# ScalarE's exponential table loaded among its input transfers, the lower bound served early, and the fourth projection tile in halves

## The chip, the cores and the metric

The kernel runs on one core of a Trainium2 chip. The metric is the device time of one execution in microseconds (us). TensorE (PE), VectorE (DVE), ScalarE (ACT), GpSimd (POOL) and SyncE (SP) each follow their own instruction stream and meet only at semaphores. Transfers are issued by SP, ScalarE and GpSimd, each on a queue of its own, and run on 16 shared DMA engines.

## What is computed

The reference is one layer of a decoder on 256 prompt tokens and 8 sample tokens (264 in all). The part that matters here is its head: a projection, and the forget gate made from one group of its columns.

```
proj = x @ w_in                      # (264, 2048) @ (2048, 10240), split into u v q f i g gate_a gate_b
p = softmax(lb_logits, axis=0); lower_bound = cumsum(p, axis=0) - p[0:1]
forget = lb + (1 - lb) * sigmoid(f)
logf = log(forget);  k = (1 - lb) * sigmoid(-f)
...                                  # gating, recurrence, output projections, norm,
...                                  # a mixture of 16 experts, norm
```

## The kernel before

**Arithmetic.** The input projection is computed as 80 column tiles of 128 columns ("tiles" below). Both operands are split into a high part in the reduced format fp32r and a low part, the rest. ScalarE makes the high part by a copy, VectorE the low part by a subtraction, and TensorE adds three products per block of 128 rows: high by high, high by low, low by high. With 16 blocks of rows (`KD`) a tile takes 48 matmuls of 264 columns, in `gemm_tile` (L662 to L664).

**The first three tiles** (`FIRST = 3`) go together, in seven chunks of rows given by `CUTS = (0, 2, 4, 6, 8, 10, 13, 16)`: five chunks of two blocks, two of three. SP issues the seven transfers of the weights (L419), ScalarE the seven of x (L1263). For each chunk ScalarE copies x (L1267), then the three tiles' weights (L1270); VectorE subtracts for x (L1464), then for the weights (L1467); TensorE waits for both and runs 18 or 27 matmuls (L843 to L845). TensorE has run 15 warm-up products before (L833).

**Tiles 3, 4, 5 and on.** SP issues each tile's weights as one transfer of 1 MB (L451), tiles 3 and 4 right behind the seven chunks, tile 5 and later ones only when TensorE has finished a tile (`gemm`). ScalarE makes the high part (`hi_part`, L1259), VectorE the low part (`lo_to`, L1455), and TensorE waits for the low part in `split_of`. Tiles 0 to 7 are the f group, whose results ScalarE takes out of the bank with two sigmoids each (L1293, L1294).

**The lower bound.** `lbl` is a parameter of 4 KB. GpSimd fetches it (L558), with two others, once all chunks of x are split (`xl_ready`). VectorE waits for all three, subtracts (L1472) and signals `lb_sub`; ScalarE answers with an exponential of 8 columns (L1320), behind the sigmoids of tile 1, and signals `lb_exp`. VectorE waits for it ahead of small set-up work (L1476 to L1484), which ends with the scales that the forget gates (L1489, L1490) and so the recurrence use. The compiler puts an ACT_TABLE_LOAD ahead of a function that the loaded table lacks.

**GpSimd** starts with masks and constants (L534 to L552) and then signals `consts`.

**Order.** Each engine's stream is written out by hand, and each engine follows its own strictly: an instruction that waits holds all behind it on that engine. Behind the projections come output projections, a norm, a router and the experts, whose weights SP streams through a ring as slots are freed.

Of the kernel before, what the change touches and what calls it, by code (L numbers as in the profile page):

```python
# [42 lines left out]
KD = D // P  # L43
# [58 lines left out]
def build(nc, x_t, w_in, ws_t, w00, b_s, lng, lnb, lbl, normg, state, woa, wob, wo, ln1g, ln1b, rw, rb,  # L102
          wg, wu, wd, ln2g, ln2b, y, st_p, st_s, v_s):
    with ExitStack() as ctx:
        def sem(name):
            return ctx.enter_context(nc.semaphore(name))
# [70 lines left out]
        def raw_of(q):  # L177

            return raw_early if q == FIRST + 1 else raw_w[q % 4]

        def lo_of(q):

            return lo_early[:, :] if q == FIRST + 1 else w_lo[q % 4][:, :]

        def chunk(buf, c):

            return buf.rearrange("p (k n) -> p k n", k=KD)[:, CUTS[c]:CUTS[c + 1], :]

        def chunk_of(buf, q, c):

            return buf[:, CUTS[c]:CUTS[c + 1], P * q:P * q + P]

        def raw_count(q):

            return q // 4 + (1 if q % 4 >= FIRST else 0)
# [79 lines left out]
        ones, _ = place("ones", [P, P])  # L275
        before = reg_qg[:, 2 * D:2 * D + P]
        quarter = before
        small, _ = place("small", [P, 648])
# [8 lines left out]
        lbw = take(4 * H).rearrange("p (a h) -> p a h", h=H)  # L287
# [6 lines left out]
        spare = take(3)  # L294
# [73 lines left out]
        x_in = [sem(f"x_in{q}") for q in range(CHUNKS - 1)]; side_in = sem("side_in"); par_in = sem("par_in"); ws_ready = sem("ws_ready"); ln1_in = sem("ln1_in"); router_in = sem("router_in")  # L368
# [4 lines left out]
        raw_in = [sem(f"raw_in{s}") for s in range(4)]; hi_ready = sem("hi_ready"); lo_ready = sem("lo_ready")  # L373
# [4 lines left out]
        lb_exp = sem("lb_exp"); lb_sub = sem("lb_sub")  # L378
# [14 lines left out]
        silu = sem("silu"); hid_ready = sem("hid_ready"); hid_tr = sem("hid_tr"); hid_ev = sem("hid_ev")  # L393
        ob_act = sem("ob_act"); ob_dve = sem("ob_dve"); weighted = sem("weighted"); pick_tr = sem("pick_tr"); pick_ev = sem("pick_ev")
        sc_mm = sem("sc_mm"); sc_ev = sem("sc_ev")
        early_mm = sem("early_mm"); early_ev = sem("early_ev"); half_in = x_in[0]; rows_in = sem("rows_in"); gain_mm = sem("gain_mm"); gain_ev = sem("gain_ev"); xg_ready = sem("xg_ready"); shift_ready = sem("shift_ready"); shift_mm = sem("shift_mm"); shift_ev = sem("shift_ev"); rank_two = sem("rank_two"); ya_ready = sem("ya_ready"); ln2q_in = sem("ln2q_in"); quarter_ready = sem("quarter_ready"); s_part = sem("s_part"); s_avg = sem("s_avg"); lob_act = sem("lob_act"); lob_dve = sem("lob_dve"); again = sem("again"); y_ready = sem("y_ready"); ys_ready = sem("ys_ready"); y_out = sem("y_out")
        zeroed = sem("zeroed"); dve_chain = sem("dve_chain")


# [16 lines left out]
        def _(sp):  # L416
# [22 lines left out]
            for q in range(FIRST, QUANTA):  # L439
                if q >= FIRST + 2:  # L440
                    sp.wait_ge(gemm, max(FIRST, tiles_done(q - 4)))
                if q < N_IN:
                    col = TILE_COL[q] * P
                    src, kk = w_in[:, col:col + P], KD
                elif q < N_IN + Q_OUT:
                    j = (q - N_IN) // 2
                    src, kk = (woa, wob)[(q - N_IN) % 2][:, 2 * P * j:2 * P * (j + 1)], H
                else:
                    j = q - N_IN - Q_OUT
                    src, kk = wo[:, P * j:P * (j + 1)], KD  # L450
                sp.dma_start(raw_of(q).rearrange("p (k n) -> p k n", k=kk),  # L451
                             src.rearrange("(k p) n -> p k n", p=P)).then_inc(raw_in[q % 4], 16)
                if q == N_IN + 8:

                    sp.dma_start(xt[:, :, :], x_t.rearrange("(k p) t -> p k t", p=P)).then_inc(x_again_in, 16)

                j = q - N_IN - Q_OUT
                if j >= 4 and j % 2 == 0 and j <= 12:
                    sp.wait_ge(gemm, N_IN + N_OUT)
                    first_unit((0, 2, 3, 4, 5)[j // 2 - 2])  # L460
# [65 lines left out]
        def _(pool):  # L526
            n = [0]
# [24 lines left out]
                link(pool.tensor_copy(out, iota_i[:, 0:k]))  # L552

            pool.nop().then_inc(consts, 1)

            pool.wait_ge(xl_ready, CHUNKS)
            with nc.allow_non_contiguous_dma("small parameters"):
                pool.dma_start(lbw[:, 0, :], lbl).then_inc(par_in, 16)  # L558
                pool.dma_start(ngain, normg).then_inc(par_in, 16)
                pool.dma_start(w00b, w00.partition_broadcast(P)).then_inc(par_in, 16)  # L560

# [86 lines left out]
        def _(pe):  # L648
            def gemm_tile(n, hi, lo, of_hi, of_lo):

                if n >= 4:
                    p = n - 4
                    if p < N_IN:
                        pe.wait_ge(act_evac, p + 1)
                    else:
                        pe.wait_ge(dve_evac, p - N_IN + 1)
                kk = len(hi)
                for k in range(kk):
                    if n == N_IN + N_OUT and k % 2 == 0:
                        pe.wait_ge(ml_ready, k // 2 + 1)  # L660
                    out = psum[n % 4][:, 0:T]
                    pe.matmul(out, hi[k], of_hi[:, k, :], start=(k == 0), stop=False)  # L662
                    pe.matmul(out, hi[k], of_lo[:, k, :], start=False, stop=False)  # L663
                    mm = pe.matmul(out, lo[k], of_hi[:, k, :], start=False, stop=(k == kk - 1))  # L664
                mm.then_inc(gemm, 1)
# [159 lines left out]

            def split_of(q, kk):

                pe.wait_ge(lo_ready, q + 1 - FIRST)
                return tuple(w.rearrange("p (k n) -> p k n", k=kk) for w in (hi_of(q), lo_of(q)))

            pe.wait_ge(warm, 1)
# [61 lines left out]
            for j in range(KD):  # L893
                n = N_IN + N_OUT + j
# [349 lines left out]
        def _(act):  # L1244
            evac_of = {}
            n = 0
# [5 lines left out]
            def hi_part(q):  # L1252

                if q < QUANTA:
                    if q >= FIRST + 2:
                        ahead = 3 if q < N_IN + Q_OUT + 2 else 2
                        act.wait_ge(gemm, tiles_done(q - ahead))
                    act.wait_ge(raw_in[q % 4], 16 * raw_count(q))
                    act.copy(hi_of(q), raw_of(q)).then_inc(hi_ready, 1)  # L1259

            for c in range(CHUNKS):
                part = slice(CUTS[c], CUTS[c + 1])
                act.dma_start(raw_x[:, part, :], x_t[P * CUTS[c]:P * CUTS[c + 1], :].rearrange("(k p) t -> p k t", p=P)).then_inc(x_in[c], 16)  # L1263
            for c in range(CHUNKS):
                part = slice(CUTS[c], CUTS[c + 1])
# [2 lines left out]
                act.wait_ge(first_in[c], 16)  # L1268
                for q in range(FIRST):
                    act.copy(chunk(hi_of(q), c), chunk_of(first_raw, q, c)).then_inc(first_hi, 1)  # L1270
            hi_part(FIRST)
            hi_part(FIRST + 1)
            def exps(lv):

# [13 lines left out]
            for n in range(N_IN):  # L1288
                name, j = evac_of[n]
                act.wait_ge(gemm, n + 1)  # L1290
                src = psum[n % 4][:, 0:T]
# [24 lines left out]
                    hi_part(n + 3)  # L1316
                if n == 1:
                    act.wait_ge(consts, 1)
                    act.wait_ge(lb_sub, 1)
                    act.activation(lbw[:, 1, :], lbw[:, 1, :], ACT.Exp).then_inc(lb_exp, 1)  # L1320
                if name == "q" and j == 3:
                    act.wait_ge(f_ready, 1)
                    act.activation(pcum[:, :, 0:NP_], pcum[:, :, 0:NP_], ACT.Ln).then_inc(logf, 1)
# [117 lines left out]
        def _(dve):  # L1441
# [8 lines left out]
            def lo_to(q_end):  # L1450

                while lo_next[0] <= min(q_end, QUANTA - 1):
                    q = lo_next[0]
                    dve.wait_ge(hi_ready, q + 1 - FIRST)
                    dve.tensor_tensor(lo_of(q), raw_of(q), hi_of(q).bitcast(F32), ALU.subtract).then_inc(lo_ready, 1)  # L1455
                    lo_next[0] += 1

            lo_next = [FIRST]
            dve.memset(ones[:, :], 1.0).then_inc(warm, 1)
            dve.memset(up[:, 0:4096 + 2 * H * BLK], 0.0).then_inc(zeroed, 1)  # L1460
            for c in range(CHUNKS):
                part = slice(CUTS[c], CUTS[c + 1])
                dve.wait_ge(xh_ready, c + 1)
                dve.tensor_tensor(x_lo[:, part, :], raw_x[:, part, :], x_hi[:, part, :].bitcast(F32), ALU.subtract).then_inc(xl_ready, 1)  # L1464
                for q in range(FIRST):
                    dve.wait_ge(first_hi, FIRST * c + q + 1)
                    dve.tensor_tensor(chunk_of(lo_first, q, c), chunk_of(first_raw, q, c), chunk(hi_of(q), c).bitcast(F32), ALU.subtract).then_inc(first_lo, 1)  # L1467
            lo_to(4)

            dve.wait_ge(par_in, 16 * 3)  # L1470
            dve.wait_ge(consts, 1)
            dve.tensor_tensor(lbw[:, 1, :], lbw[:, 0, :], lbw[:, 0, :], ALU.subtract).then_inc(lb_sub, 1)  # L1472
            dve.wait_ge(lb_exp, 1)
            for j in range(P // BLK):
                rows = slice(BLK * j, BLK * j + BLK)
# [192 lines left out]
            for r in range(Q_OUT):  # L1668
# [12 lines left out]
                for f in range(2):  # L1681
                    n = N_IN + 2 * r + f
# [37 lines left out]
            for j in range(KD):  # L1720
                n = N_IN + N_OUT + j
# [391 lines left out]
```

## Time and profile before

| | |
|---|---|
| median of 3 runs | 1659.89 us (1658.84 to 1660.66) |
| profiled execution, own time | 1660.23 us |
| its span on the core | 1658.5 us |
| TensorE busy | 1594.6 us (96%) |
| VectorE busy | 684.4 us (41%) |
| ScalarE busy | 392.1 us (24%) |
| GpSimd busy | 46.1 us (3%) |
| DMA | 543.87 MB, 328 GB/s on average |

The span is what the trace covers; the execution's own time is 1.73 us longer. Busy time of TensorE is modelled, since matmuls are pipelined, so 96% doesn't mean that it runs at its peak. Times in a timeline count from the span's start; what stands in brackets is the idle time of the engine just before the instruction, and what ended it.

### The profile page before, as it was taken

How to read it: one execution, taken by the hardware profiler on the slowest of the kernel's cores; microseconds unless marked ns; L12 is line 12 of the kernel's file. 1: busy time of each engine (PE TensorE's matmuls, PEld its weight loads, DVE VectorE, ACT ScalarE, POOL GpSimd, SP SyncE). 2: the span in 40 equal slices, each digit the busy share in tenths (PEclk: the TensorE clock that was granted, in tenths of full speed). 3: DMA queues.
4: the chain of work that ended last, by engine and by line, in shares of the span. 5: the costliest groups of instructions: out<-in, count | busy, mean ns of one | idle time of the engine just before them, and what ended most of it. 6: DMA issues, size and time to landing. Idle time of an engine off the chain costs nothing.

```text
span 1658.5 us, 25058 instructions
## 1 busy us (share of the span) xinstructions
PE 1594.6 (96%) x11140; PEld 1060.3 (64%) x11140; DVE 684.4 (41%) x1023; ACT 392.1 (24%) x419; POOL 46.1 (3%) x85
## 2 busy tenths in 40 slices
PE   8999999999999999999998998998998999889998
PEld 8999999999999999973532423434334234225334
DVE  7437688657575665544520110111021021102726
ACT  6444555533454333320000000000000000000002
POOL 2000000022000000000000000000000000000000
PEclk9999999999999999999999999999999999999998
DMA  9676566589566769889999999999999999999995
GB/s 263 186 224 169 157 201 175 157 251 309 167 174 185 231 178 328 254 321 406 423 430 430 432 434 431 431 432 431 432 433 433 431 432 432 430 432 432 432 413 176
DMA packets 240708, 543.87 MB, mean 328 GB/s; under 512 B 5072, under 2 KB 218144, under 8 KB 227312
## 3 DMA queue, kind: packets, MB, share of 16 engines
q1 hardware_dynamic: 233536, 524.93, 83.3%
q0 software_dynamic: 4896, 15.49, 2.8%
q10 hardware_dynamic: 2192, 2.20, 0.4%
q8 instruction: 69, 1.13, 0.3%
q14 instruction: 15, 0.12, 0.0%
HBM read 535.65 MB, written 6.95 MB: 327 GB/s over the span
## 4 chain that ended last, share of the span: by engine, by line
PE 78%; DMA 19%; DVE 1%; ACT 1%; issue 0%; SPq 0%; DVEq 0%; ACTq 0%
PE bank L980 16%; PE bank L662 13%; PE bank L663 12%; PE bank L664 12%; PE bank L1074 10%; DMA ring_low<-wu 10%; DMA ring_high<-wu 8%; PE bank L943 5%; PE bank L1152 3%; DMA ring_low<-w_in 2%; PE bank L1108 1%; PE bank L1060 1%; PE bank L716 0%; PE bank L1146 0%; PE bank L997 0%
## 5 line engine op out<-in xcount | busy, mean ns | idle before, releaser
L664 PE MATMUL bank<-x_hi,w_lo 128*128 128x264 f32 x1216 | 344.3, 283 | 0.0
L662 PE MATMUL bank<-x_hi,w_hi 128*128 128x264 f32 x1200 | 343.7, 286 | 0.0
L663 PE MATMUL bank<-x_lo,w_hi 128*128 128x264 f32 x1200 | 340.0, 283 | 0.0
L980 PE MATMUL bank<-ring_low,reg_pk 128*64 128x512 f32 x1248 | 280.8, 603 | 27.7 <-DMA ring_low<-wu 26.6
L1455 DVE TENSOR_TENSOR w_lo<-ring_low,w_hi 128x2048 fp32r<-128x2048 f32 x107 | 244.8, 2289 | 139.5 <-ACT w_hi L1259 139.0
L1259 ACT CAST w_hi<-ring_low 128x2048 fp32r<-128x2048 f32 x107 | 203.7, 1903 | 140.3 <-PE bank L664 92.3
L664 PEld LDWEIGHTS bank<-x_hi,w_lo 128*128 128x128 f32 x1216 | 228.0, 187 | 0.0
L662 PEld LDWEIGHTS bank<-x_hi,w_hi 128*128 128x128 f32 x1200 | 226.0, 188 | 2.1 <-issue 1.7
L663 PEld LDWEIGHTS bank<-x_lo,w_hi 128*128 128x128 f32 x1200 | 226.2, 189 | 0.1
L980 PEld LDWEIGHTS bank<-ring_low,reg_pk 128*64 128x64 f32 x1248 | 88.0, 139 | 213.6 <-issue 170.6
L980 PE MATMUL bank<-ring_high,reg_pk 128*64 128x512 f32 x768 | 175.7, 612 | 22.0 <-DMA ring_high<-wu 19.3
L1896 DVE TENSOR_TENSOR xt<-xt,bank 128x512 f32<-128x512 f32 x15 | 10.3, 687 | 358.8 <-ACT xt L1383 358.8
L1074 PE MATMUL bank<-ring_high,xt 128*64 128x512 f32 x704 | 154.0, 593 | 0.0
L980 PEld LDWEIGHTS bank<-ring_high,reg_pk 128*64 128x64 f32 x768 | 55.1, 141 | 140.3 <-issue 105.4
L1074 PEld LDWEIGHTS bank<-ring_high,xt 128*64 128x64 f32 x704 | 49.9, 137 | 97.4 <-issue 96.6
L1383 ACT ACTIVATE xt<-bank 128x512 f32<-128x512 f32 x15 | 9.0, 597 | 420.5 <-PE bank L980 420.5
L943 PEld LDWEIGHTS bank<-pick,reg_uv 128*128 128x128 f32 x768 | 87.1, 192 | 7.5 <-issue 7.3
L943 PE MATMUL bank<-pick,reg_uv 128*128 128x128 f32 x768 | 89.6, 276 | 0.0
L1900 DVE COPY xt<-bank 64x512 f32<-64x512 f32 x14 | 9.6, 683 | 169.1 <-PE bank L1074 169.0
L662 PE MATMUL bank<-m_hi,w_hi 128*128 128x264 f32 x256 | 73.0, 285 | 0.0
L662 PE MATMUL bank<-y_parts,w_hi 128*128 128x264 f32 x256 | 72.8, 284 | 0.0
L663 PE MATMUL bank<-y_parts,w_hi 128*128 128x264 f32 x256 | 72.5, 283 | 0.0
(385 smaller groups left out, 1699.1 us busy)
## 6 DMA issues: line engine op xcount, KB each, us to landing
ring_high<-wd SPq DMA_DIRECT2D x21, 4096.0 KB, 30.0
ring_low<-wg SPq DMA_DIRECT2D x21, 4096.0 KB, 29.9
ring_low<-w_in SPq DMA_DIRECT2D x76, 1024.0 KB, 5.8
ring_high<-wu SPq DMA_DIRECT2D x14, 4096.0 KB, 23.7
ring_low<-wu SPq DMA_DIRECT2D x14, 4096.0 KB, 25.5
ring_low<-wd SPq DMA_DIRECT2D x7, 4096.0 KB, 31.6
ring_high<-wg SPq DMA_DIRECT2D x7, 4096.0 KB, 31.5
ring_low<-wo SPq DMA_DIRECT2D x16, 1024.0 KB, 7.0
```

Of the source, the lines that this page charges most:

```text
L662: pe.matmul(out, hi[k], of_hi[:, k, :], start=(k == 0), stop=False)
L663: pe.matmul(out, hi[k], of_lo[:, k, :], start=False, stop=False)
L664: mm = pe.matmul(out, lo[k], of_hi[:, k, :], start=False, stop=(k == kk - 1))
L943: mm = pe.matmul(b[:, P * j:P * (j + 1)], x1[:, tt, P * k:P * k + P], pick[:, tt, :, :].rearrange("p a s -> p (a s)"), start=(tt == 0), st ...
L980: mm = pe.matmul(psum[2 * a + part][64 * half:64 * half + 64, :], xg[:, k, CAP * a:CAP * a + CAP], wt[:, kk, 512 * half:512 * half + 512], ...
L1060: mm = pe.transpose(psum[2 * a][:, P * j:P * (j + 1)], hid[:, P * j:P * (j + 1)], ident[:, :])
L1074: mm = pe.matmul(psum[4 + nn // 2][64 * (nn % 2):64 * (nn % 2) + 64, :], hidt[:, k % 4, k // 4, :], wt[:, kk, 512 * nn:512 * nn + 512], st ...
L1108: mm = pe.matmul(psum[4 + c % 2][64 * half:64 * half + 64, 0:256], hidt[:, k % 4, k // 4, :], wt[:, k, 256 * half:256 * half + 256], start ...
L1152: pe.matmul(psum[6 + b % 2][:, :], pick_t[:, P * tt:P * tt + P], ob[:, 512 * nn:512 * nn + 512], start=True, stop=True).then_inc(sc_mm, 1)
L1259: act.copy(hi_of(q), raw_of(q)).then_inc(hi_ready, 1)
L1455: dve.tensor_tensor(lo_of(q), raw_of(q), hi_of(q).bitcast(F32), ALU.subtract).then_inc(lo_ready, 1)
L1896: dve.tensor_tensor(hid_out, hid_out, by_hidden(psum[2 * a + 1][:, :]), ALU.mult).then_inc(hid_ready, 1)
```

## The change

It has three parts. First, ScalarE issues three of its seven x transfers, then runs an exponential of one column into a spare word, and then issues the other four; the table load comes with it. Second, the lower bound: GpSimd fetches `lbl` right behind its constants, on a semaphore of its own (`lb_in`); VectorE subtracts behind chunk 1 of the first tiles; ScalarE takes the exponential behind chunk 2. Third, tile 3 is transferred, copied and subtracted in two halves of 8 blocks, and TensorE waits for the second low half ahead of block 8.

```diff
@@ sync
-                sp.dma_start(raw_of(q).rearrange("p (k n) -> p k n", k=kk),
-                             src.rearrange("(k p) n -> p k n", p=P)).then_inc(raw_in[q % 4], 16)
+                dst, src = raw_of(q).rearrange("p (k n) -> p k n", k=kk), src.rearrange("(k p) n -> p k n", p=P)
+                if q == FIRST:
+                    sp.dma_start(dst[:, 0:KD // 2, :], src[:, 0:KD // 2, :]).then_inc(half_raw, 16)
+                    sp.dma_start(dst[:, KD // 2:KD, :], src[:, KD // 2:KD, :]).then_inc(raw_in[q % 4], 16)
+                else:
+                    sp.dma_start(dst, src).then_inc(raw_in[q % 4], 16)
@@ gpsimd
             pool.nop().then_inc(consts, 1)
+            with nc.allow_non_contiguous_dma(reason="small"):
+                pool.dma_start(lbw[:, 0, :], lbl).then_inc(lb_in, 16)
 
             pool.wait_ge(xl_ready, CHUNKS)
             with nc.allow_non_contiguous_dma("small parameters"):
-                pool.dma_start(lbw[:, 0, :], lbl).then_inc(par_in, 16)
@@ tensor, gemm_tile
                 for k in range(kk):
+                    if n == FIRST and k == KD // 2:
+                        pe.wait_ge(lo_ready, 1)
@@ tensor, split_of
-                pe.wait_ge(lo_ready, q + 1 - FIRST)
+                if q == FIRST:
+                    pe.wait_ge(first_lo, FIRST * CHUNKS + 1)
+                else:
+                    pe.wait_ge(lo_ready, q + 1 - FIRST)
@@ scalar
             for c in range(CHUNKS):
                 part = slice(CUTS[c], CUTS[c + 1])
+                if c == 3:
+                    act.wait_ge(warm, 1)
+                    act.activation(spare[:, 0:1], ones[:, 0:1], ACT.Exp)
                 act.dma_start(raw_x[:, part, :], x_t[P * CUTS[c]:P * CUTS[c + 1], :].rearrange("(k p) t -> p k t", p=P)).then_inc(x_in[c], 16)
@@
                 for q in range(FIRST):
                     act.copy(chunk(hi_of(q), c), chunk_of(first_raw, q, c)).then_inc(first_hi, 1)
-            hi_part(FIRST)
+                if c == 2:
+                    act.wait_ge(lb_sub, 1)
+                    act.activation(lbw[:, 1, :], lbw[:, 1, :], ACT.Exp).then_inc(lb_exp, 1)
+            act.wait_ge(half_raw, 16)
+            act.copy(by_rows(hi_of(FIRST))[:, 0:KD // 2, :], by_rows(raw_of(FIRST))[:, 0:KD // 2, :]).then_inc(first_hi, 1)
+            act.wait_ge(raw_in[FIRST % 4], 16 * raw_count(FIRST))
+            act.copy(by_rows(hi_of(FIRST))[:, KD // 2:KD, :], by_rows(raw_of(FIRST))[:, KD // 2:KD, :]).then_inc(hi_ready, 1)
             hi_part(FIRST + 1)
@@
                 if n == 1:
                     act.wait_ge(consts, 1)
-                    act.wait_ge(lb_sub, 1)
-                    act.activation(lbw[:, 1, :], lbw[:, 1, :], ACT.Exp).then_inc(lb_exp, 1)
@@ vector
-            lo_next = [FIRST]
+            lo_next = [FIRST + 1]
@@
                     dve.tensor_tensor(chunk_of(lo_first, q, c), chunk_of(first_raw, q, c), chunk(hi_of(q), c).bitcast(F32), ALU.subtract).then_inc(first_lo, 1)
+                if c == 1:
+                    dve.wait_ge(lb_in, 16)
+                    dve.tensor_tensor(lbw[:, 1, :], lbw[:, 0, :], lbw[:, 0, :], ALU.subtract).then_inc(lb_sub, 1)
+            dve.wait_ge(first_hi, FIRST * CHUNKS + 1)
+            dve.tensor_tensor(by_rows(lo_of(FIRST))[:, 0:KD // 2, :], by_rows(raw_of(FIRST))[:, 0:KD // 2, :], by_rows(hi_of(FIRST))[:, 0:KD // 2, :].bitcast(F32), ALU.subtract).then_inc(first_lo, 1)
+            dve.wait_ge(hi_ready, 1)
+            dve.tensor_tensor(by_rows(lo_of(FIRST))[:, KD // 2:KD, :], by_rows(raw_of(FIRST))[:, KD // 2:KD, :], by_rows(hi_of(FIRST))[:, KD // 2:KD, :].bitcast(F32), ALU.subtract).then_inc(lo_ready, 1)
             lo_to(4)
 
-            dve.wait_ge(par_in, 16 * 3)
+            dve.wait_ge(par_in, 16 * 2)
             dve.wait_ge(consts, 1)
-            dve.tensor_tensor(lbw[:, 1, :], lbw[:, 0, :], lbw[:, 0, :], ALU.subtract).then_inc(lb_sub, 1)
             dve.wait_ge(lb_exp, 1)
```

`by_rows` gives a tile's buffer as 16 blocks. The order of ScalarE's instructions at its start, before (`reg_uv` holds the raw x, `ring_low` the raw weights):

```order
L1263 DMA reg_uv<-x_t 128x2x264 x5
L1263 DMA reg_uv<-x_t 128x3x264 x2
L1267 ACT_TABLE_LOAD
L1267 CAST x_hi<-reg_uv 128x528 [waits x_in0]
L1270 CAST w_hi_60<-ring_low 128x256 [waits first_in0]
```

and with the change (`small` holds the spare word):

```order
L1280 DMA reg_uv<-x_t 128x2x264 x3
L1279 ACT_TABLE_LOAD
L1279 ACTIVATE small<-ones 128x1 [waits warm]
L1280 DMA reg_uv<-x_t 128x2x264 x2
L1280 DMA reg_uv<-x_t 128x3x264 x2
L1284 CAST x_hi<-reg_uv 128x528 [waits x_in0]
```

The table load has moved from behind the seventh transfer to behind the third, and a one-column exponential has come with it. VectorE around the border of chunks 1 and 2 of the first tiles, with the change (`small` holds the lower bound):

```order
L1485 TENSOR_TENSOR x_lo<-reg_uv,x_hi 128x528 [waits xh_ready]
L1488 TENSOR_TENSOR lo_first<-ring_low,w_hi_60 128x2x128 [waits first_hi]
L1488 TENSOR_TENSOR lo_first<-ring_low,w_hi_61 128x2x128 [waits first_hi]
L1488 TENSOR_TENSOR lo_first<-ring_low,w_hi_62 128x2x128 [waits first_hi]
L1491 TENSOR_TENSOR small<-small 128x8 [waits lb_in]
L1485 TENSOR_TENSOR x_lo<-reg_uv,x_hi 128x528 [waits xh_ready]
L1488 TENSOR_TENSOR lo_first<-ring_low,w_hi_60 128x2x128 [waits first_hi]
```

The row that waits for `lb_in` is new there; before, it stood behind tile 4's subtraction. ScalarE from its work on tiles 3 and 4 to tile 5, before (`w_early` and `w_hi` are high parts, `reg_pk` takes the sigmoids):

```order
L1259 CAST w_early_63<-ring_low 128x2048 [waits raw_in3]
L1259 CAST w_early_64<-reg_uv 128x2048 [waits raw_in0]
L1293 ACT_TABLE_LOAD
L1293 ACTIVATE reg_pk<-bank 128x264 [waits gemm]
L1294 ACTIVATE reg_pk<-bank 128x264
L1293 ACTIVATE reg_pk<-bank 128x264 [waits gemm]
L1294 ACTIVATE reg_pk<-bank 128x264
L1320 ACT_TABLE_LOAD [waits lb_sub]
L1320 ACTIVATE small<-small 128x8 [waits consts]
L1293 ACT_TABLE_LOAD
L1293 ACTIVATE reg_pk<-bank 128x264 [waits gemm]
```

and with the change:

```order
L1292 CAST w_early_63<-ring_low 128x1024 [waits half_raw]
L1294 CAST w_early_63<-ring_low 128x1024 [waits raw_in3]
L1273 CAST w_early_64<-reg_uv 128x2048 [waits raw_in0]
L1316 ACT_TABLE_LOAD
L1316 ACTIVATE reg_pk<-bank 128x264 [waits gemm]
L1317 ACTIVATE reg_pk<-bank 128x264
L1316 ACTIVATE reg_pk<-bank 128x264 [waits gemm]
L1317 ACTIVATE reg_pk<-bank 128x264
L1316 ACTIVATE reg_pk<-bank 128x264 [waits gemm,consts]
```

The copy of tile 3 stands there in two, and two table loads and the exponential are gone from among the sigmoids.

## Rows read from the trace of the kernel before

**Rows 1.** The page: span, the chain that ended last by engine

```profile
span 1658.5 us, 25058 instructions
...
PE 78%; DMA 19%; DVE 1%; ACT 1%; issue 0%; SPq 0%; DVEq 0%; ACTq 0%
```

**Rows 2.** Timeline of PE, 0 to 28 us: start, length, what, idle before and releaser

```profile
1.10 5.04 PE L833 MATMUL bank<-ones 128*128 128x128 f32 x30 [1.10 <-DVE ones L1459]
8.62 0.36 PE L843 MATMUL bank<-x_hi,w_hi 128*128 128x264 f32 x1 [2.48 <-DVE lo_first L1467]
...
26.02 0.28 PE L845 MATMUL bank<-x_hi,lo_first 128*128 128x264 f32 x1
27.10 0.39 PE L662 MATMUL bank<-x_hi,w_early 128*128 128x264 f32 x1 [0.80 <-DVE w_lo L1455]
```

**Rows 3.** Timeline of ScalarE, 0 to 48 us (ACTq is its queue)

```profile
0.79 4.65 ACTq L1263 DMA_DIRECT2D reg_uv<-x_t  x7
5.47 1.28 ACT L1267 ACT_TABLE_LOAD   x1 [5.47 <-issue]
6.76 0.63 ACT L1267 CAST x_hi<-reg_uv 128x528 fp32r<-128x528 f32 x1
...
16.21 0.85 ACT L1267 CAST x_hi<-reg_uv 128x792 fp32r<-128x792 f32 x1 [1.16 <-DMA reg_uv<-x_t]
...
22.81 1.91 ACT L1259 CAST w_early<-ring_low 128x2048 fp32r<-128x2048 f32 x1 [2.06 <-DMA ring_low<-w_in]
...
30.54 1.28 ACT L1320 ACT_TABLE_LOAD   x1
...
33.91 1.91 ACT L1259 CAST w_hi<-ring_low 128x2048 fp32r<-128x2048 f32 x1
```

**Rows 4.** Timeline of VectorE, 0 to 48 us

```profile
7.43 0.71 DVE L1464 TENSOR_TENSOR x_lo<-reg_uv,x_hi 128x528 fp32r<-128x528 f32 x1 [1.57 <-ACT x_hi L1267]
8.05 1.09 DVE L1467 TENSOR_TENSOR lo_first<-ring_low,w_hi 128x256 fp32r<-128x256 f32 x3
...
10.69 0.70 DVE L1464 TENSOR_TENSOR x_lo<-reg_uv,x_hi 128x528 fp32r<-128x528 f32 x1
...
28.00 2.29 DVE L1455 TENSOR_TENSOR lo_early<-reg_uv,w_early 128x2048 fp32r<-128x2048 f32 x1 [0.95 <-ACT w_early L1259]
...
32.07 1.05 DVE L1476 COPY ring_high<-ring_high 32x192 f32<-32x192 f32 x4 [1.70 <-ACT small L1320]
...
36.24 2.28 DVE L1455 TENSOR_TENSOR w_lo<-ring_low,w_hi 128x2048 fp32r<-128x2048 f32 x1
```

**Rows 5.** Timeline of GpSimd, 0 to 25 us

```profile
8.46 0.40 POOL L552 CAST small<-small 128x4 f32<-128x4 int32 x1
20.83 0.71 POOL L558 DMA_DIRECT2D small<-lbl  x1 [11.97 <-DVE x_lo L1464]
```

**Rows 6.** DMA issues: count, KB, us from issue to landing

```profile
reg_uv<-x_t ACTq DMA_DIRECT2D x1, 264.0 KB, 4.9
...
small<-lbl POOLq DMA_DIRECT2D x1, 4.0 KB, 4.1
...
reg_uv<-ln1b POOLq DMA_DIRECT2D x1, 8.0 KB, 2.0
...
ring_high<-ln1b POOLq DMA_DIRECT2D x1, 8.0 KB, 6.8
```

**Rows 7.** Timeline of ScalarE at the end of the program

```profile
1654.12 0.69 ACT L1427 ACTIVATE reg_qg<-bank,small 128x512 f32<-128x512 f32 x1 [1.44 <-PE bank L1197]
1654.48 1.32 ACTq L1437 DMA_DIRECT2D y<-xt  x2
```

**Rows 8.** Timeline of PE around two idle stretches in the expert part

```profile
1017.57 6.64 PE L980 MATMUL bank<-ring_low,reg_pk 128*64 128x512 f32 x22 [2.63 <-DMA ring_low<-wu]
...
1493.49 7.09 PE L980 MATMUL bank<-ring_low,reg_pk 128*64 128x512 f32 x32 [2.63 <-DMA ring_low<-wu]
```

**Rows 9.** Busy us by stretch, granted clock, DMA share, GB/s last

```profile
1017.00:1022.00 5.00, 4.43 (x14) 1.41 (x16) 0.00 (x0) 0.00 (x0) 0.00 (x0) 0.66 0.99 426
```

More of the change, by code:

```diff
@@ L191, in chunk_of, with by_rows @@
             return buf[:, CUTS[c]:CUTS[c + 1], P * q:P * q + P]
+        def by_rows(buf):
+            return buf.rearrange("p (k n) -> p k n", k=KD)
         def raw_count(q):
@@ L395, in build @@
         sc_mm = sem("sc_mm"); sc_ev = sem("sc_ev")
-        early_mm = sem("early_mm"); early_ev = sem("early_ev"); half_in = x_in[0]; rows_in = sem("rows_in"); gain_mm = sem("gain_mm"); gain_ev = sem("gain_ev"); xg_ready = sem("xg_ready"); shift_ready = sem("shift_ready"); shift_mm = sem("shift_mm"); shift_ev = sem("shift_ev"); rank_two = sem("rank_two"); ya_ready = sem("ya_ready"); ln2q_in = sem("ln2q_in"); quarter_ready = sem("quarter_ready"); s_part = sem("s_part"); s_avg = sem("s_avg"); lob_act = sem("lob_act"); lob_dve = sem("lob_dve"); again = sem("again"); y_ready = sem("y_ready"); ys_ready = sem("ys_ready"); y_out = sem("y_out")
+        early_mm = sem("early_mm"); early_ev = sem("early_ev"); half_in = x_in[0]; half_raw = sem("half_raw"); lb_in = sem("lb_in"); rows_in = sem("rows_in"); gain_mm = sem("gain_mm"); gain_ev = sem("gain_ev"); xg_ready = sem("xg_ready"); shift_ready = sem("shift_ready"); shift_mm = sem("shift_mm"); shift_ev = sem("shift_ev"); rank_two = sem("rank_two"); ya_ready = sem("ya_ready"); ln2q_in = sem("ln2q_in"); quarter_ready = sem("quarter_ready"); s_part = sem("s_part"); s_avg = sem("s_avg"); lob_act = sem("lob_act"); lob_dve = sem("lob_dve"); again = sem("again"); y_ready = sem("y_ready"); ys_ready = sem("ys_ready"); y_out = sem("y_out")
         zeroed = sem("zeroed"); dve_chain = sem("dve_chain")
```

## The prediction

> **What bounds the kernel now.** I read the chain that ended last first: TensorE carries 78% of it and DMA 19% [rows 1]. The DMA share lies in the experts' part, but its transfers start when TensorE frees slots, so a shift of TensorE at the head should travel through to the end. All that the change touches lies in the first 40 us. There I read TensorE's timeline for idle stretches [rows 2]. It has two behind the warm-up: 2.48 us before the first projection matmul, which starts at 8.62, and 0.80 us before tile 3, at 27.10. In between it never stops: from 8.62 to 26.02 there are 143 steps of 0.122 us. So the whole stake is the start at 8.62, the 0.80 us, and whatever new gap appears between.
>
> The start hangs on ScalarE. Its queue issues seven transfers from 0.79 to 5.44, the table load runs from 5.47 to 6.75, and the first copy of x follows at 6.76 [rows 3]. That x landed at 0.79 + 4.9 = 5.69 [rows 6], so the table load holds the start for about 1.07 us. Tile 3 hangs on its transfer: the copy starts at 22.81, behind a wait for it [rows 3].
>
> **Part one, the table load among the transfers.** Does ScalarE's queue stand still while the engine loads the table? No row shows a table load with a transfer behind it. The nearest one is at the end: a transfer is issued at 1654.48 while an activation runs from 1654.12 to 1654.81 [rows 7]. So I take it that queue and engine overlap. The load then lies beside the issues, done by about 4.5, and the first copy starts at 5.75 instead of 6.76: a gain of 1.0 us, first matmul at 7.6. The other bound is a queue that stands still for the load's 1.28 us and 0.2 for the activation: issues until 6.95, first copy 0.2 us later than before, and four x transfers 1.5 us late.
>
> **Part two, the early lower bound.** It adds a wait. VectorE, done with chunk 1, now waits for the 4 KB of `lbl`, and queued behind it are the subtractions of chunk 2, for which TensorE waits. Before, VectorE took up chunk 2 at 10.69 [rows 4]; with the earlier start it arrives between 9.7 and 10.7. When does `lbl` land? GpSimd ends its constants at 8.86 [rows 5]; two semaphore steps on, I put the issue at 9.0. The same transfer took 4.1 us in the kernel before, issued at 20.83 while weights were streaming [rows 5, 6]. The fastest small transfer of GpSimd took 2.0 us, the slowest that is not among the experts' weights 6.8 [rows 6]. I take 4.1, because it is the same transfer beside the same kind of stream, though at 9.0 two other queues are full instead of one. It lands at T = 13.1, with bounds 11.0 and 15.8.
>
> From T on: 0.2 us for the subtraction of 8 columns, then x's subtraction. In chunk 0 that one started at 7.43 [rows 4] and TensorE at 8.62 [rows 2], so 1.2 us. Chunk 2 starts on TensorE at T + 1.4 = 14.5. The two chunks before it hold 36 matmuls, 4.4 us, done at 12.0. TensorE idles about 2.5 us there, and **this wait takes the place of the wait removed from the start**. Whether the start came at 7.6 or 8.8 no longer matters. The remaining 108 matmuls take 108 x 0.122 = 13.1 us. VectorE needs 1.6 us per two-block chunk (7.43 to 10.69 were two, [rows 4]), TensorE 2.2, so it isn't caught again. Chunk 5 is wanted at 14.5 + 3 x 2.2 = 21.1; its x landed at 16.2 [rows 3] and would still be in time 1.5 us later. The third tile ends at T + 14.5 = 27.6.
>
> **The lower bound's other end.** ScalarE loses two table loads of 1.28 us among the sigmoids, one of them at 30.54 [rows 3], and VectorE its wait of 1.70 us at 32.07 [rows 4]. Neither is on the path. Tile 5's low part was ready at 36.24 + 2.28 = 38.5 [rows 4], and TensorE, at 5.8 us per tile, wanted it at 27.10 + 11.7 = 38.8. So nothing is gained there now, but a margin of only 0.3 us would have eaten a much earlier start. With the change VectorE starts its set-up at 30.3, where tile 4's subtraction ends [rows 4], and tile 5 is ready at 36.8. I cost this at nothing; its cover is VectorE's new slack.
>
> **Part three, halves of tile 3.** If even the first half landed with the whole at 22.8, its copy would take 1.1 us and its subtraction 1.2 (by the slope between the shapes of chunk 0 and of the whole tile, [rows 3, 4]), ready at 25.1. That is before TensorE wants it in any case here, so the 0.80 us go. The second half is wanted 2.9 us later. The extra issue on SP lies ahead of tile 4 alone, whose low part is wanted 5.8 us after tile 3 starts, at 33.4, and was ready at 30.3 [rows 4].
>
> **Sum.** Tile 3 starts at T + 14.5 = 27.6 instead of 27.10, so +0.5 us. The gain of 1.0 at the start and of 0.8 at tile 3 is used up by a wait worth 2.3. Against the profiled execution, 1660.23 us (span 1658.5 and 1.73 around it), that is 1660.7. The median of the three runs lies 0.34 lower, so I forecast 1660.4.
>
> A rule speaks for more. By the same rows, the answer depends on T alone: T - 12.6 us. The Trainium skill, DMA: Bandwidth & Descriptors, section "Anatomy of one DMA — SWDGE (gpsimd) path", gives such a transfer a fixed cost of about 2.0 us plus its bytes over 436 GB/s; the trace's 4.1 us for this very transfer disagrees, its 2.0 us for the fastest one agrees. By the page the sum would be about 1.6 us of gain.
>
> **Rivals.**
> - *The bound lands in time.* If `lbl` takes 2.0 us as the fastest row [rows 6], T = 11.0, chunk 2 starts at 12.4 and tile 3 at 25.5: -1.6 us, 1658.3. At T below 10.6 it would be the whole -1.8. For it: the row. Against it: the same transfer's own 4.1. By the page's rule named above this is what happens. Were the queue to stand still for the table load as well, this gain would be less. Chance 0.22.
> - *The clock falls in the new gap.* The trace has 15 idle stretches of TensorE of 2.48 to 2.63 us, the first at 8.62 [rows 2], the last before 1493.49 [rows 8]. After 7 of them the granted clock fell to 0.50, that is from 2.4 to 1.2 GHz, as after the one before 1017.57 [rows 8], after 8 it stayed at 1.00; shorter ones never did it. A fall cost 5 x (1 - 0.66) = 1.7 us of TensorE's work [rows 9]. My gap of 2.5 us is on the edge. With the fall: +2.2 us, 1662.1. Chance 0.18.
> - *Slower in a measurable way.* One mechanism, at VectorE's wait behind chunk 1: `lbl` lands late because two full queues share the DMA engines with it, and the longer gap brings the clock down as well. At the slowest row, 6.8 us, T = 15.8: +3.2 for the wait and +1.7 for the clock, 1664.8. It decides from T = 14.2 on, a landing of 5.2 us. For it: the DMA engines are busy all through this stretch, and several small transfers of GpSimd took over 5 us. Against it: 4.1 beside a similar stream. Chance 0.11.
> - *The change doesn't do what it says*: the exponential's table is followed by another load at the first copy. The order of instructions shows none, and my sum doesn't rest on the start. Chance 0.02, time as forecast.
>
> **How the numbers follow.** The forecast itself has 0.47: +0.5 us. About 0.2% (3.3 us) is what a measurement of this kernel can tell from no change. The forecast, the clock case and the case in time all lie within it: 0.86 with a little taken off for the tails. Slower gets the third rival, 0.11. Faster by over 3.3 us would need almost twice what both removed waits hold; 0.03 for a shift in the experts' part that no row foretells. The three runs before spread over 1.8 us. The range goes from the case in time less 0.6 to the clock case plus 1.6, 1657.7 to 1663.7, which takes in `lbl` at its late bound of 15.8 without a fall of the clock.
>
> **What would show it.** In the profile after: the table load of ScalarE near 3, its first copy of x near 5.8, TensorE's first projection matmul near 7.6 (part one). VectorE's 8-column subtraction near 13, with a wait for the `lbl` transfer before it, and a gap of about 2.5 us on TensorE before chunk 2 (part two). No gap before tile 3, which starts near 27.6, and none before tiles 4 and 5. The prediction is wrong if TensorE starts tile 3 before 26.5 or after 29, if the queue's issues stretch to 7, or if the end moves by something other than the start of tile 3.

## The result, and the profile after

Over 11 runs each, the changed kernel takes 1662.96 us (1661.37 to 1665.80) and the kernel before 1659.39 us (1657.76 to 1662.70). The ratio is 1.0022, 95% interval 1.0014 to 1.0029: slower by 3.6 us. The forecast was 1660.4 us, no measurable change; the time lies inside the range, near its upper end, but the change is clear of the noise and tile 3 starts later than the 29 us that the prediction named as a sign of being wrong. One of the eleven executions of e9 below took 1993.89 us at a granted clock of 0.75 and is left out of its median and ratio.

The page of the changed kernel: its span, and the chain that ended last.

```profile
span 1659.5 us, 25060 instructions
...
PE 78%; DMA 19%; DVE 1%; issue 1%; ACT 0%; POOL 0%; DVEq 0%; POOLq 0%; ACTq 0%
```

The chain has not changed its make-up [rows 1]. The profiled execution took 1661.37 us, the fastest of the eleven, so sizes are read from the head's rows, not from its span. TensorE's timeline in the head:

```profile
7.49 0.36 PE L857 MATMUL bank<-x_hi,w_hi 128*128 128x264 f32 x1
...
15.92 0.36 PE L857 MATMUL bank<-x_hi,w_hi 128*128 128x264 f32 x1 [3.66 <-DVE lo_first L1488]
...
30.61 0.28 PE L673 MATMUL bank<-x_hi,w_early 128*128 128x264 f32 x1
```

The first matmul stands at 7.49 instead of 8.62 [rows 2], so the early table load brought 1.1 us. But chunk 2, the first that is queued behind the new wait, starts only at 15.92, after 3.66 us of idle time, and tile 3 at 30.61 instead of 27.10: 3.5 us late, and without a gap of its own. ScalarE:

```profile
0.79 1.55 ACTq L1280 DMA_DIRECT2D reg_uv<-x_t  x3
2.37 1.28 ACT L1279 ACT_TABLE_LOAD   x1 [2.37 <-issue]
2.43 1.51 ACTq L1280 DMA_DIRECT2D reg_uv<-x_t  x2
3.66 0.20 ACT L1279 ACTIVATE small<-ones 128x1 f32<-128x1 f32 x1
3.97 1.38 ACTq L1280 DMA_DIRECT2D reg_uv<-x_t  x2
5.64 0.63 ACT L1284 CAST x_hi<-reg_uv 128x528 fp32r<-128x528 f32 x1 [1.77 <-DMA reg_uv<-x_t]
...
14.85 0.21 ACT L1290 ACTIVATE small<-small 128x8 f32<-128x8 f32 x1 [3.53 <-DVE small L1491]
...
21.85 1.05 ACT L1292 CAST w_early<-ring_low 128x1024 fp32r<-128x1024 f32 x1
...
36.73 1.91 ACT L1273 CAST w_hi<-ring_low 128x2048 fp32r<-128x2048 f32 x1 [5.18 <-DMA ring_low<-w_in]
```

The table load runs from 2.37 to 3.65 while the queue issues the next transfers from 2.43 on. The whole set of issues ends at 5.35, earlier than the 5.44 before [rows 3]. The copy of the first x stands at 5.64. From chunk 2's weights (done at 11.3) to 14.85 ScalarE waits as well. The last row, tile 5's copy at 36.73, now waits for a transfer that SP could issue only when the third tile was done. VectorE:

```profile
8.63 0.71 DVE L1485 TENSOR_TENSOR x_lo<-reg_uv,x_hi 128x528 fp32r<-128x528 f32 x1 [0.58 <-ACT x_hi L1284]
...
14.65 0.17 DVE L1491 TENSOR_TENSOR small<-small 128x8 f32<-128x8 f32 x1 [4.30 <-DMA small<-lbl]
14.73 0.70 DVE L1485 TENSOR_TENSOR x_lo<-reg_uv,x_hi 128x528 fp32r<-128x528 f32 x1
...
30.25 1.04 DVE L1503 COPY ring_high<-ring_high 32x192 f32<-32x192 f32 x4
...
38.67 2.29 DVE L1476 TENSOR_TENSOR w_lo<-ring_low,w_hi 128x2048 fp32r<-128x2048 f32 x1 [4.18 <-ACT w_hi L1273]
```

It is done with chunk 1 at 10.35 and takes up the 8-column subtraction at 14.65; 4.30 us of waiting, for `lbl`. The reason lies on GpSimd, whose last constant and whose issue of `lbl` are

```profile
8.52 0.19 POOL L560 CAST small<-small 128x4 f32<-128x4 int32 x1
9.41 0.71 POOL L564 DMA_DIRECT2D small<-lbl  x1 [0.70 <-POOL small L560]
```

and in the transfer (KB, us from issue to landing):

```profile
small<-lbl POOLq DMA_DIRECT2D x1, 4.0 KB, 5.2
```

9.41 + 5.2 = 14.6. TensorE's granted clock, the third number from the end of each row:

```profile
12.00:14.00 2.00, 0.25 (x3) 0.04 (x1) 0.00 (x0) 0.00 (x0) 0.00 (x0) 1.00 1.07 362
...
16.00:18.00 2.00, 2.00 (x15) 2.00 (x16) 2.00 (x7) 2.00 (x7) 0.00 (x0) 0.85 1.11 345
18.00:20.00 2.00, 2.00 (x11) 2.00 (x11) 2.00 (x6) 2.00 (x5) 0.00 (x0) 0.50 1.20 291
20.00:22.00 2.00, 2.00 (x15) 2.00 (x15) 2.00 (x5) 2.00 (x5) 0.00 (x0) 0.80 1.19 295
22.00:24.00 2.00, 2.00 (x19) 2.00 (x18) 2.00 (x4) 1.85 (x2) 0.80 (x2) 1.00 1.18 290
```

It falls from 1.00 to 0.50 (2.4 to 1.2 GHz) within chunk 2 and comes back near 21. Last, TensorE's waits in us over the whole span:

```profile
PE bank L857 <- DVE lo_first L1488: 3.7, 1, 3.7
...
PE bank L781 <- DVE reg_qg L1635: 0.3, 1, 0.3
```

The second lies at 370 us, long behind the head: TensorE waits there until VectorE has copied the previous result out of the bank that the next products go to (L1608 before, L1635 here). In the kernel before this wait took 1.3 us:

```profile
368.24 0.49 PE L770 MATMUL bank<-ring_high 128*128 128x128 f32 x2 [1.33 <-DVE reg_qg L1608]
```

It is 0.3 here. It was 0.3 to 1.0 in the nine profiles of the experiments that had it (all but e3 and e9), with an early head as with a late one, so it can't be read as an answer to the head.

### The profile page after: what moved, and what is told of

It reads as the page before. It is cut to its first block, busy times and chain, and to the rows that moved or that the text cites. A ratio compares the mean times of both kernels' runs of the same rounds, so it can differ in the third digit from the quotient of the medians.

```text
span 1659.5 us, 25060 instructions
## 1 busy us (share of the span) xinstructions
PE 1597.4 (96%) x11140; PEld 1063.2 (64%) x11140; DVE 684.1 (41%) x1024; ACT 389.5 (23%) x419; POOL 46.0 (3%) x85
## 4 chain that ended last, share of the span: by engine, by line
PE 78%; DMA 19%; DVE 1%; issue 1%; ACT 0%; POOL 0%; DVEq 0%; POOLq 0%; ACTq 0%
PE bank L994 15%; PE bank L673 13%; PE bank L674 12%; PE bank L675 12%; DMA ring_low<-wu 11%; PE bank L1088 10%; DMA ring_high<-wu 8%; PE bank L957 5%; PE bank L1166 3%; PE bank L1122 1%; DMA ring_low<-w_in 1%; PE bank L1074 1%; PE bank L727 0%; PE bank L1160 0%; PE bank L1011 0%
## 5 line engine op out<-in xcount | busy, mean ns | idle before, releaser
L673 PE MATMUL bank<-y_parts,w_hi 128*128 128x264 f32 x256 | 72.9, 285 | 0.0
L674 PE MATMUL bank<-m_lo,w_hi 128*128 128x264 f32 x256 | 72.6, 284 | 0.0
```

## The experiments

**Theory W**: VectorE's wait for `lbl` behind chunk 1, and the clock's fall behind the gap that it makes, are the whole loss; parts one and three gain 1.8 us. **Theory H**: the head loses through its transfers, by x issued late or by the halves. **Theory L**: the loss arises in the experts' part whatever the head does. The kernel before ran beside each group of experiments; its median there is 1659.62 (e1, e2, e4, e5), 1659.75 (e3, e6, e7, e8) and 1660.05 us (e9 to e11).

### e1: the lower bound as before

Against the changed kernel, on GpSimd, VectorE and ScalarE:

```diff
             pool.nop().then_inc(consts, 1)
-            with nc.allow_non_contiguous_dma(reason="small"):
-                pool.dma_start(lbw[:, 0, :], lbl).then_inc(lb_in, 16)

             pool.wait_ge(xl_ready, CHUNKS)
             with nc.allow_non_contiguous_dma("small parameters"):
+                pool.dma_start(lbw[:, 0, :], lbl).then_inc(par_in, 16)
...
-                if c == 1:
-                    dve.wait_ge(lb_in, 16)
-                    dve.tensor_tensor(lbw[:, 1, :], lbw[:, 0, :], lbw[:, 0, :], ALU.subtract).then_inc(lb_sub, 1)
...
             lo_to(4)

-            dve.wait_ge(par_in, 16 * 2)
+            dve.wait_ge(par_in, 16 * 3)
             dve.wait_ge(consts, 1)
+            dve.tensor_tensor(lbw[:, 1, :], lbw[:, 0, :], lbw[:, 0, :], ALU.subtract).then_inc(lb_sub, 1)
```

ScalarE's exponential goes back in the same way, from behind chunk 2 to behind tile 1's sigmoids.

> Parts one and three of the change alone: the early table load and tile 3 in halves, the lower bound served as in the kernel before. Theory W (VectorE's wait for lbl and the clock fall behind it are the whole loss): first projection matmul near 7.5, no gap at chunk 2, tile 3 starts at 25.0 to 25.5 instead of 27.10; then tile 5's low part, ready near 38.5 as in the kernel before, is wanted at 37.0, so TensorE waits about 1.5 us there; the sum is -0.3 us against before (-0.1 to -0.6). Theory H (the head loses by the transfers, halves or delayed x): tile 3 starts at 27 or later. Theory L (the loss arises in the experts' part, whatever the head does): the head gains and the time is still 2 us or more above before.

1659.29 us, ratio 0.9999 (0.9990 to 1.0008). TensorE around tile 3 and tile 5:

```profile
25.29 0.28 PE L672 MATMUL bank<-x_hi,w_early 128*128 128x264 f32 x1
...
38.62 0.39 PE L672 MATMUL bank<-x_hi,w_hi 128*128 128x264 f32 x1 [1.57 <-DVE w_lo L1474]
```

The gap at chunk 2 is gone, tile 3 starts at 25.29, and 1.57 us of the 1.8 gained are lost again 13 us later, where tile 5's low part is late. So H falls: with early table load and halves, but without the early bound, the head is faster than before. L falls too. It shows as well what part two is for: without it an earlier start is worth nothing.

### e2: the early bound alone

This is the kernel before with part two of the change and nothing else; on VectorE, for one:

```diff
+                if c == 1:
+                    dve.wait_ge(lb_in, 16)
+                    dve.tensor_tensor(lbw[:, 1, :], lbw[:, 0, :], lbw[:, 0, :], ALU.subtract).then_inc(lb_sub, 1)
```

> Part two alone: lbl fetched behind the constants, VectorE's wait behind chunk 1, exponential behind chunk 2; table load and tile 3 as in the kernel before. Theory W: lbl lands near 14.5, chunk 2 starts near 15.9 as with the whole change; the gap before it is about 1.2 us shorter (2.5 instead of 3.7), since the first matmul starts at 8.6. Tile 3 starts at 29.2 without a fall of the clock, at 30.7 with one, so +2.1 or +3.6 us. Theory H: as fast as before, within 0.5 us, since parts one and three would carry the loss.

1661.68 us, ratio 1.0013 (1.0004 to 1.0022), +2.1 us. TensorE's chunk 2 and tile 3, and the clock behind chunk 2's start:

```profile
16.18 0.36 PE L844 MATMUL bank<-x_hi,w_hi 128*128 128x264 f32 x1 [2.96 <-DVE lo_first L1469]
...
29.36 0.28 PE L663 MATMUL bank<-x_hi,w_early 128*128 128x264 f32 x1
```

```profile
16.00:18.00 2.00, 1.82 (x15) 1.85 (x16) 2.00 (x7) 2.00 (x7) 0.00 (x0) 1.00 1.10 348
18.00:20.00 2.00, 2.00 (x19) 2.00 (x18) 2.00 (x6) 2.00 (x5) 0.00 (x0) 1.00 1.19 291
```

`lbl` took 5.3 us from 9.56. Chunk 2 starts within 0.3 us of where it does in the change, though the first matmul came 1.1 us later. After this gap of 2.96 us the clock stayed at 1.00, and the median is what theory W gives without a fall. The profiled execution itself took 1663.23 us, though: the end of a single execution doesn't tell whether the clock fell in the head.

### e4 and e5: nobody waits for the transfer

e4 fetches `lbl` as GpSimd's first instruction; e5 leaves the fetch where the change has it and moves the waits.

e5 on ScalarE and VectorE, against the changed kernel:

```diff
-                if c == 2:
-                    act.wait_ge(lb_sub, 1)
-                    act.activation(lbw[:, 1, :], lbw[:, 1, :], ACT.Exp).then_inc(lb_exp, 1)
             act.wait_ge(half_raw, 16)
...
+            act.wait_ge(lb_sub, 1)
+            act.activation(lbw[:, 1, :], lbw[:, 1, :], ACT.Exp).then_inc(lb_exp, 1)
             hi_part(FIRST + 1)
...
-                if c == 1:
-                    dve.wait_ge(lb_in, 16)
-                    dve.tensor_tensor(lbw[:, 1, :], lbw[:, 0, :], lbw[:, 0, :], ALU.subtract).then_inc(lb_sub, 1)
+            dve.wait_ge(lb_in, 16)
+            dve.tensor_tensor(lbw[:, 1, :], lbw[:, 0, :], lbw[:, 0, :], ALU.subtract).then_inc(lb_sub, 1)
             dve.wait_ge(first_hi, FIRST * CHUNKS + 1)
```

> The whole change, but GpSimd fetches lbl as its first instruction, ahead of masks and constants. Theory W: issued near 0.5, before the queues are full, it lands before 8, VectorE doesn't wait behind chunk 1, the clock stays at 1.00, tile 3 starts at 25.0 to 25.5. Tile 5 is wanted at 37.0 and ready near 36.8, so no wait of more than 0.3 there; -1.8 us against before (-1.3 to -2.2). Theory H: tile 3 at 27 or later. Theory L: still 2 us or more above before. If a small transfer takes 5 us wherever it is issued, it still lands in time here.

> The whole change, but VectorE waits for lbl only behind all seven chunks, and ScalarE takes the exponential behind tile 3's second half. The transfer is issued as in the change, near 9.4, and lands near 14.6. Theory W: nobody waits for it; tile 3 starts at 25.0 to 25.5, -1.8 us against before (-1.3 to -2.2), the same as with lbl fetched first. If it is the transfer itself that does harm and not the wait for it (a rival within W), this run stays slower than the one with lbl fetched first. Theory H and theory L as there.

e4: 1658.14 us, ratio 0.9990 (0.9981 to 0.9999). e5: 1657.89 us, 0.9991 (0.9982 to 1.0000). Tile 3 starts at 25.50 and 25.18; neither has a gap at chunk 2, at tile 3 or at tile 5. In e4 the transfer took long as well,

```profile
small<-lbl POOLq DMA_DIRECT2D x1, 4.0 KB, 6.0
```

but from 1.33 on, and the subtraction ran at 10.43 without a wait. In e5, VectorE's 8-column subtraction and tile 5's subtraction:

```profile
21.68 0.16 DVE L1489 TENSOR_TENSOR small<-small 128x8 f32<-128x8 f32 x1
...
34.25 2.29 DVE L1475 TENSOR_TENSOR w_lo<-ring_low,w_hi 128x2048 fp32r<-128x2048 f32 x1
```

The transfer stands where it does in the change and does no harm; the wait for it does. Tile 5 is ready at 36.5, where e1 had it at 38.6. That is part two's worth, 1.6 us, when it costs nothing.

### e6 and e7: the halves

e6 is e5 with tile 3 whole; e7 is the kernel before with tile 3 in halves.

> The kernel with the wait behind all chunks, but tile 3 transferred, copied and subtracted whole as before. The first three tiles end at 25.2 as there; tile 3's low part hangs on its transfer, lands at 22.8, so it starts near 27.1 after a gap of 1.9 us. Time as before, 0.0 us (-0.3 to +0.3): an earlier start without the halves is worth nothing. If the halves were not what carries it, tile 3 would start near 25.2 and the time be 1.7 us under before.

> Part three alone: the kernel before with tile 3 in halves; the table load behind the transfers, the lower bound as before. First matmul at 8.6, tile 3 at 26.3 (26.1 by the starts) instead of 27.10; then tile 5's low part, ready at 38.5, is wanted at 37.9, so a gap of 0.5 us. Sum -0.3 us against before (0 to -0.6).

e6: 1659.26 us, ratio 0.9997 (0.9988 to 1.0006). TensorE's tile 3:

```profile
27.20 0.39 PE L667 MATMUL bank<-x_hi,w_early 128*128 128x264 f32 x1 [1.58 <-DVE w_lo L1463]
```

e7: 1659.40 us, ratio 0.9996 (0.9987 to 1.0005); tile 3 starts at 26.30, and TensorE waits for tile 5's low part 0.7 us. Both times are as expected, though the gap in e6 is 1.58 us and not 1.9. So part three alone (e7), parts one and three (e1), and parts one and two with the late wait (e6) bring nothing that can be measured, and part two alone (e2) costs 2.1 us; part one alone was not run. The three together, with the wait in another place, are worth 1.5 to 2.4 us.

### e3 and e9: the clock

On TensorE, against the changed kernel; e9 has 18 in place of 10:

```diff
             for c in range(CHUNKS):
+                if c == 2:
+                    for _ in range(10):
+                        pe.matmul(psum[7][:, 0:P], ones[:, :], ones[:, :], start=True, stop=True)
```

> The whole change, with ten more products of the warm-up kind on TensorE ahead of chunk 2, into a bank that nothing reads. They fill the 3.7 us in which TensorE waits behind chunk 1, and nothing else is altered. Theory W with the clock: the clock stays at 1.00, chunk 2 still starts near 15.9 (the wait for lbl is not shortened), tile 3 starts near 29.1 instead of 30.6, so +2.0 us against before instead of +3.6. If the clock is not part of the loss: tile 3 still near 30.6 and +3.6.

> The whole change with 18 filling products instead of 10 ahead of chunk 2: the ten took 2.4 us (0.24 each) and left TensorE idle for 2.15 us, and the clock fell all the same. 18 take 4.3 us from the end of chunk 1 near 11.9 to 16.2, so almost no idle time is left. If idle time before chunk 2 is what brings the clock down, it stays at 1.00, chunk 2 starts at 15.9 to 16.3, tile 3 at 29.1 to 29.5 and the time is +2.0 us against before and 1.5 under the change run beside it. If the fall comes whatever TensorE does there, tile 3 stays near 31.

e3 missed its aim. I had taken 0.33 us for a product from the warm-up (5.04 us for 15, [rows 2]). That mean mixes two speeds: in the trace of the kernel before, the warm-up's products start 0.43 us apart up to 4.04 us and 0.22 us apart behind it. The ten took 2.40:

```profile
11.77 2.40 PE L852 MATMUL bank<-ones 128*128 128x128 f32 x20
16.32 0.36 PE L860 MATMUL bank<-x_hi,w_hi 128*128 128x264 f32 x1 [2.15 <-DVE lo_first L1491]
```

The clock fell all the same (18 to 20 us: 0.50), and its profile has tile 3 at 31.00. Yet the median is 1661.42 us, ratio 1.0010 (1.0001 to 1.0019), 1.7 us above before, and that profiled execution took no more than 1661.56. The head doesn't explain so short a time. e9 closed the gap:

```profile
12.16 4.18 PE L852 MATMUL bank<-ones 128*128 128x128 f32 x36
...
29.27 0.28 PE L673 MATMUL bank<-x_hi,w_early 128*128 128x264 f32 x1
```

```profile
18.00:20.00 2.00, 2.00 (x19) 2.00 (x18) 2.00 (x6) 2.00 (x6) 0.00 (x0) 1.00 1.19 295
```

1660.69 us, ratio 1.0009 (0.9999 to 1.0018), and no fall. Tile 3 is at 29.27, 1.3 us ahead of the change, with `lbl` as late as ever (issued at 9.47, 5.2 us). The three profiles with the wait and idle time next to it (the change, e10, e3) have the fall, the one without idle time doesn't, and its time is 3.1 us under that of e10. That speaks for TensorE's idle time as the cause. It is not shown beyond doubt: e9 has one profile, and in e2 the clock stayed up behind 2.96 us of idle time.

### e10 and e11: the change and the late wait once more

> The change once more, beside the filled one on the same chip. Theory W: lbl takes 5 to 6 us, chunk 2 starts near 15.9 after a gap of 3.7 us, the clock falls to 0.50 for 3.4 us, tile 3 starts near 30.6, +3.6 us against before (3.0 to 4.0). If the fall of the clock was chance in the one profile, this profile shows it at 1.00 and tile 3 near 29.

> The kernel with the wait behind all chunks once more, to see whether it beats both kernels: -1.8 us against before (-1.3 to -2.2), 5.4 under the change.

e10: 1663.77 us, ratio 1.0023 (1.0013 to 1.0033). `lbl` took 5.5 us from 9.69, and the gap is 4.51 us. This time the clock fell inside the gap already:

```profile
12.00:14.00 2.00, 0.00 (x0) 0.00 (x0) 0.00 (x0) 0.00 (x0) 0.00 (x0) 0.99 1.07 368
14.00:16.00 2.00, 0.00 (x0) 0.00 (x0) 0.79 (x3) 0.59 (x2) 0.00 (x0) 0.50 1.07 357
...
18.00:20.00 2.00, 2.00 (x11) 2.00 (x11) 2.00 (x6) 2.00 (x5) 0.00 (x0) 0.50 1.20 290
```

Tile 3 starts at 31.58. By tile 3 it would be 4.4 us above before; the median is 3.7. e9 beside it is 3.1 us faster, of which the profiles explain 2.3 (31.58 - 29.27). e11: 1657.61 us, ratio 0.9986 (0.9977 to 0.9995), 2.4 us under before and 6.2 under the change. The kernel with the late wait beats both.

### e8: the landing at another time

GpSimd issues `lbl` when chunk 3 is split; otherwise e5.

> The kernel with the wait behind all chunks, but GpSimd issues lbl only when chunk 3 is split, near 13.5. A probe of the landing alone. If two full queues of other transfers beside it make the landing long (5.2 us at 9.4, 4.1 at 20.8 when only one is left), it takes 4.8 to 5.5 us here. If it is the place in the program, it falls steadily and takes about 4.7. Nobody waits for it: tile 3 near 25.2.

Issued at 12.95, it took

```profile
small<-lbl POOLq DMA_DIRECT2D x1, 4.0 KB, 6.4
```

longer than either reading had it. The time, 1656.27 us, is a single run. Over all profiles: 6.0 us issued at 1.33, 5.2 to 5.5 at 9.2 to 9.8 (eight profiles), 6.4 at 12.95, and 4.1 to 4.2 at 20.8 to 20.9 (three). While x and the weights both stream, it never took under 5.2; with x done, about 4.1. That fits two full queues beside it. Another small transfer speaks against the place in the program as the reason. `normg`, 4 KB too, is GpSimd's next transfer behind `lbl` both in e5 and in the change, and is issued when all of x is split; the rows are those of e5, then those of the change:

```profile
20.67 0.55 POOL L568 DMA_DIRECT2D small<-normg  x1 [10.64 <-DVE x_lo L1484]
small<-normg POOLq DMA_DIRECT2D x1, 4.0 KB, 4.5
...
23.20 0.55 POOL L568 DMA_DIRECT2D small<-normg  x1 [13.07 <-DVE x_lo L1485]
small<-normg POOLq DMA_DIRECT2D x1, 4.0 KB, 2.2
```

Issued 2.5 us later it took half the time, and both landed near 25, just when the stream of weights runs out (the DMA share in e5 is 1.19 from 22 to 24 us and 0.25 from 24 to 26). So the time of a small transfer here follows the traffic beside it. How much of `lbl`'s 5.2 us is due to the second queue, no run shows.

## Why the prediction was right, and by how much it was off

*What bounds, and where the stake lies.* Right in the main. In all but two experiments (e3 and e9) the time against before lies within 0.8 us of what the start of tile 3 and the gap at tile 5 give. By tile 3's start in the profile (us) and the median against before (e8, a single run, is left out):

| | tile 3 starts | later gap at tile 5 | time against before |
|---|---|---|---|
| before | 27.10 | none | |
| e5 | 25.18 | none | -1.7 |
| e11 (e5 again) | 25.27 | none | -2.4 |
| e1 | 25.29 | 1.6 | -0.3 |
| e4 | 25.50 | none | -1.5 |
| e7 | 26.30 | 0.7 | -0.35 |
| e6 | 27.20 | none | -0.5 |
| e9 | 29.27 | none | +0.6 |
| e2 | 29.36 | none | +2.1 |
| the change | 30.61 | none | +3.6 |
| e3 | 31.00 | none | +1.7 |
| e10 (the change again) | 31.58 | none | +3.7 |

*The start.* Right: queue and engine overlap; 7.6 forecast, 7.49 measured. The bound of a queue that stands still is refuted by 2.43 against 2.37.

*The wait takes the gain's place.* Right as a mechanism, and mis-sized in the term T. I had `lbl` issued at 9.0 and landed at 13.1; it was issued at 9.41 and landed at 14.6. Of the 1.5 us, 0.4 are the issue: between GpSimd's last constant, which ended at 8.71, and the transfer lie 0.70 us, for which I gave 0.14. The other 1.1 are the landing. I took the same transfer's own row, 4.1 us [rows 6], and named the fuller queues without giving them a price.

*From T on.* T + 1.4 for chunk 2 held: 14.6 + 1.3 = 15.9. The 108 matmuls took 14.7 us instead of 13.1, since the clock fell (13.2 in e2, where it didn't); my gap of 2.5 us was 3.66. The fall's price of 1.7 was right to 0.2. My reading that shorter idle stretches never bring the clock down was wrong: e3 has a fall behind 2.15 us, and at the end of the kernel before the granted clock falls as well (0.84 in 1648 to 1650 us, 0.50 in 1650 to 1652), where the longest idle stretch ahead of it was 1.32 us, at 1640.

*Tile 5 and tile 3.* Both right. I had costed the early bound's saving at nothing in this kernel and said that the margin of 0.3 us would eat an earlier start: e1 lost 1.57 us there. The halves took the gap at tile 3 away.

*The likeliest case.* So what came was the third rival: late landing and fallen clock, from T = 14.2 on. It was given 0.11, with its price at the bound; at T = 14.6 its own formula gives 2.0 + 1.7 = 3.7 us, and 3.6 was measured. The step that failed is the landing in T, the choice of 4.1 us between 2.0 and 6.8, which measured 5.2; with it fell "no measurable change", and the prediction's own sign came true, tile 3 after 29. That the time lies inside the range is partly luck: the upper end was set for `lbl` at its latest without a fall of the clock, or for the fall without a late `lbl`, and what came was both, at sizes that happen to fit under it. The kernel before also came out 0.5 us lower over its eleven runs (1659.39) than over the three that the forecast started from. The Trainium skill, DMA: Bandwidth & Descriptors, section "Anatomy of one DMA — SWDGE (gpsimd) path", has a fixed cost of about 2.0 us. That was further off still for `lbl`, which never came under 4.1 in these runs; with the stream nearly over it agrees, 2.2 us for `normg`.

What stays open is the rest of the program. In every profile the shift that tile 3 and the gap at tile 5 give is kept to 0.1 us until 346 us. Then two places alter it, and neither follows the head. Around the wait at 368 us (L770), which was longer in the profile of before than in any other, every other profile gains 0.4 to 1.5 us. And from the first to the last of these rows of the experts' part, two of before, then two of the change, the kernel before takes 668.2 us and the change 666.1:

```profile
860.96 7.50 PE L1152 MATMUL bank<-xt 128*128 128x512 f32 x15
...
1529.18 1.71 PE L997 MATMUL bank<-reg_uv,ident 16*128 16x128 f32 x16
...
863.36 7.93 PE L1166 MATMUL bank<-xt 128*128 128x512 f32 x16
...
1529.50 1.71 PE L1011 MATMUL bank<-reg_uv,ident 16*128 16x128 f32 x16
```

By the same rows it takes 667.3 us in e10, which is the change once more, 668.2 in e2, 666.3 in e9 and 665.8 in e3. So a single profile's end is no measure of the head, and part of what e3 and e9 are short of (+1.7 against +3.9, +0.6 against +2.2) may be chance there. That their filling products do something further behind is not excluded; no run varied the later parts by themselves. The intervals of the change, 2.3 to 4.8 us here and 2.2 to 5.5 in e10, and the same order in two groups of runs don't need it.

## What to carry to other kernels

A small transfer that is moved to an earlier place also moves the wait for it: put the wait where the data is certain to be there, not where the arithmetic would like it, and price its landing among the queues that are full at that moment. A gap of a few us in TensorE's stream costs more than its length when the clock falls with it, as it did in three of the four profiles with such a gap and the wait in this place. And an earlier start pays only as far as the next margin, which is worth measuring first.

## What the runs showed of the hardware

- ScalarE's queue issues transfers while the engine loads a table: 2.43 against 2.37 to 3.65.
- The 4 KB transfer of `lbl` by GpSimd took 4.1 to 6.4 us in the head, at least 5.2 while two other queues streamed; 4 KB of `normg` took 2.2 us with the stream nearly over.
- From the end of GpSimd's last constant to its issue of `lbl` lie 0.70 us.
- TensorE's clock fell to 0.50 after 2.15 us of idle time in e3, where filling products came ahead, but not after 2.96 us in e2. The length of one gap doesn't decide it alone.
- A product of the warm-up kind (128 x 128) took 0.43 us in the first 3 us of the kernel before and 0.22 us from 4.19 us on.
